# Values stationary in the attention mix of a two-layer decoder trunk, with the probabilities scaled on GpSimd first

## The reference

```
proj = h @ w_in + b_in            # 16 query heads, 2 key/value heads, head size 64
s = q k^T / 8 over the own and the previous block of 128 keys, masked to the band
mx = max(max(s), sink);  p = exp(s - mx)
p = p / (sum(p) + exp(sink - mx))
o = p v                            # per head 128 queries x 64
z = o @ w_out + b_out;  h = h + rmsnorm(z);  then rmsnorm(h) goes to the MLP
```

## Time and profile before

| | us |
|---|---|
| median of 3 runs (1154.96 to 1155.65) | 1155.17 |
| the profiled execution | 1156.1 |
| its span, first to last instruction | 1154.3 |
| attention steps: first `scores` to the first matmul of `ffn(1)` | 651.3 to 785.3 |

### The profile page before, as it was taken

How to read it: one execution, slowest core, us unless ns; L and a number is a source line. 1 busy time by engine, 2 the same in 40 slices (tenths; PEclk the granted TensorE clock), 3 DMA queues, 4 the chain that set the end, 5 groups by cost and what they waited for, 6 DMA issues and landing times.

```text
span 1154.3 us, 15362 instructions
## 1 busy us (share of the span) xinstructions
PE 1132.9 (98%) x5833; PEld 956.6 (83%) x5833; DVE 543.5 (47%) x834; ACT 431.9 (37%) x748; POOL 13.3 (1%) x22
## 2 busy tenths in 40 slices
PE   6999999999999999999999999999999999999997
PEld 6888888889888888888889988889888888888886
DVE  5434457864344344423356476646444434423344
ACT  6411225554323223323245266654332332423242
POOL 0000000000000000000000000000000000000000
PEclk9999999999999999999999999999999999999999
DMA  8232221422332333222262542002433233212241
GB/s 230 69 89 78 60 85 55 128 74 73 109 95 87 109 92 90 73 68 96 91 183 73 144 95 73 2 1 74 125 93 109 86 96 109 73 55 91 93 144 73
DMA packets 142984, 105.06 MB, mean 91 GB/s; under 512 B 22183, under 2 KB 130913, under 8 KB 142945
## 3 DMA queue, kind: packets, MB, share of 16 engines
q1 hardware_dynamic: 142944, 104.52, 30.8%
HBM read 102.41 MB, written 2.10 MB: 91 GB/s over the span
## 4 chain that ended last, share of the span: by engine, by line
PE 92%; DVE 4%; ACT 3%; DMA 1%; issue 1%; SPq 0%; DVEq 0%; ACTq 0%
PE ps L1312 18%; PE ps L1313 18%; PE ps L1314 18%; PE ps L1548 6%; PE ps L1549 6%; PE ps L1547 6%; PE ps L1651 2%; PE ps L1492 2%; PE ps L1494 2%; PE ps L1493 2%; PE ps L1377 1%; PE ps L1379 1%; PE ps L1378 1%; PE ps L1624 1%; PE ps L1635 1%; PE ps L1448 1%
## 5 line engine op out<-in xcount | busy, mean ns | idle before, releaser
L1312 PE MATMUL ps<-act_hi,w_hi 128*128 128x512 f32 (+1 forms) x1072 | 388.0, 362 | 1.4 <-DVE act_lo L848 1.4
L1313 PE MATMUL ps<-act_lo,w_hi 128*128 128x512 f32 (+1 forms) x1072 | 385.8, 360 | 0.0
L1314 PE MATMUL ps<-act_hi,w_lo 128*128 128x512 f32 (+1 forms) x1072 | 385.6, 360 | 0.0
L1312 PEld LDWEIGHTS ps<-act_hi,w_hi 128*128 128x128 f32 x1072 | 203.3, 190 | 33.4 <-DVE act_lo L848 2.2
L1314 PEld LDWEIGHTS ps<-act_hi,w_lo 128*128 128x128 f32 x1072 | 203.3, 190 | 30.1
L1313 PEld LDWEIGHTS ps<-act_lo,w_hi 128*128 128x128 f32 x1072 | 203.4, 190 | 29.7
L1547 PE MATMUL ps<-w_hi 128*128 128x512 f32 x288 | 112.0, 389 | 0.0
L1548 PE MATMUL ps<-w_lo,w_hi 128*128 128x512 f32 x288 | 112.0, 389 | 0.0
L1549 PE MATMUL ps<-w_hi,w_lo 128*128 128x512 f32 x288 | 112.0, 389 | 0.0
L671 ACT ACTIVATE arena<-ps,vecs 128x512 f32<-128x512 f32 x44 | 34.3, 780 | 188.9 <-PE ps L1314 188.9
L496 ACT CAST w_hi<-raw 128x1024 fp32r<-128x1024 f32 x71 | 73.4, 1047 | 84.3 <-PE ps L1314 45.0
(11 more groups left out here) (167 smaller groups left out, 1205.5 us busy)
## 6 DMA issues: line engine op xcount, KB each, us to landing
raw<-in_f_w_up SPq DMA_DIRECT2D x88, 512.0 KB, 4.5
raw<-in_f_w_down SPq DMA_DIRECT2D x44, 512.0 KB, 3.3
raw<-in_m_w_in SPq DMA_DIRECT2D x24, 512.0 KB, 3.8
raw<-in_m_w_out SPq DMA_DIRECT2D x8, 512.0 KB, 3.3
raw<-in_a_w_in SPq DMA_DIRECT2D x16, 256.0 KB, 4.4
raw<-in_a_w_out SPq DMA_DIRECT2D x16, 256.0 KB, 4.7
h<-in_x SPq DMA_DIRECT2D x4, 512.0 KB, 5.1
out<-h SPq DMA_DIRECT2D x3, 512.0 KB, 2.6
```

Source lines behind the costliest of these rows:

```text
L1312: nc.tensor.matmul(dst, lh, rh, start=(i == 0), stop=False)
L1313: nc.tensor.matmul(dst, lh, rl, start=False, stop=False)
L1314: last = nc.tensor.matmul(dst, ll, rh, start=False, stop=(i == n - 1))
```

## The change

`mix` is turned round: the values (128 keys x 64, a weight load with 64 columns) are stationary, and the transposed probabilities of two heads that share a key group move, 256 columns. The output of key group g goes to partitions 64g to 64g+63 of bank 4, which is the layout of `act_hi`; per step and key block there are two matmuls, g = 0 and g = 1. Queries are now along the row, so the inverse can't be applied behind the mix; POOL multiplies the probabilities by it before they are transposed, and `turn_probs` waits for POOL (`pn_done`) where it waited for ACT (`p_done`). `mixed_hi` (ACT) and `mixed_lo` (DVE) write bank 4 straight to the pair; `o_tok`, `normalised` and the 8 "out" turns are gone. `out` waits for `o_lo` of its own step, so it is listed one step earlier, `y`, `post` and `pre` keep their steps, and the norm turns lie in other steps than before. On DVE `y` now stands ahead of `masked_max`. At the end one list is left (s = 16), in which `mix(15)` stands behind `out(3, 0)`.

```diff
             if c < NB:
-                return {0: [("out", c - 2, 3), ("y", c - 2), ("turn", "out", c - 1, 0)],
-                        1: [("out", c - 1, 0), ("post", c - 2), ("turn", "out", c - 1, 1)],
-                        2: [("out", c - 1, 1), ("pre", c - 2), ("turn", "norm", c - 2, 0)],
-                        3: [("out", c - 1, 2), ("turn", "norm", c - 2, 1)]}[i]
-            if i == 0:
-                return [("out", NB - 2, 3), ("y", NB - 2), ("turn", "out", NB - 1, 0),
-                        ("turn", "out", NB - 1, 1)]
-            return [("out", NB - 1, 0), ("out", NB - 1, 1), ("post", NB - 2), ("out", NB - 1, 2),
-                    ("pre", NB - 2), ("turn", "norm", NB - 2, 0), ("turn", "norm", NB - 2, 1),
-                    ("out", NB - 1, 3), ("y", NB - 1), ("post", NB - 1), ("pre", NB - 1),
-                    ("turn", "norm", NB - 1, 0), ("turn", "norm", NB - 1, 1)]
+                return {0: [("y", c - 2), ("out", c - 1, 0), ("turn", c - 3, 1)],
+                        1: [("out", c - 1, 1), ("post", c - 2)],
+                        2: [("out", c - 1, 2), ("pre", c - 2)],
+                        3: [("out", c - 1, 3), ("turn", c - 2, 0)]}[i]
+            return [("y", NB - 2), ("out", NB - 1, 0), ("mix", AT_STEPS - 1), ("turn", NB - 3, 1),
+                    ("post", NB - 2), ("out", NB - 1, 1), ("pre", NB - 2), ("out", NB - 1, 2),
+                    ("turn", NB - 2, 0), ("turn", NB - 2, 1), ("out", NB - 1, 3), ("y", NB - 1),
+                    ("post", NB - 1), ("pre", NB - 1), ("turn", NB - 1, 0), ("turn", NB - 1, 1)]
...
+            for s in range(AT_STEPS):
+
+                b, lo = s % 2, P if s < ASTEPS else 0
+                pool.wait_ge(inv_done, s + 1)
+                nc.gpsimd.tensor_tensor(sc[:, b, :, lo:], sc[:, b, :, lo:],
+                                        asm[:, b, 5].unsqueeze(2).to_broadcast([P, AG, 2 * P - lo]),
+                                        ALU.mult).then_inc(pn_done, 1)
...
                                [:, :, lo:]).then_inc(pt_done, 1)
 
+            def mixed_hi(s):
+
+                blk, n = s // ASTEPS, s % ASTEPS
+                act.wait_ge(pv_mm, s + 1)
+                nc.scalar.copy(act_hi[:, 2 * n:2 * n + 2, blk * P:(blk + 1) * P],
...
+                elif w[0] == "mix":
+                    mixed_hi(w[1])
 
             probs(0)
-            for s in range(AT_STEPS + 2):
-                if 1 <= s <= AT_STEPS and s != ASTEPS + 1:
+            for s in range(AT_STEPS):
+                if s >= 1:
                     turned(s - 1)
-                if s >= AT_STEPS:
-
-                    for w in sorted(WORK[s], key=lambda w: s == AT_STEPS and w[0] == "y"):
-                        work(w)
-                        if w == ("post", NB - 2):
-                            split_hi(G_UP[1])
-                            split_hi(G_UP[1] + 1)
-                        if w == ("turn", "norm", NB - 2, 1):
-                            split_hi(G_UP[1] + 2)
-                        if w == ("post", NB - 1):
-                            split_hi(G_UP[1] + 3)
-                    continue
-                if s >= 1:
                     for w in WORK[s - 1]:
                         if w[0] in ("y", "post"):
                             work(w)
                 for k in OUT_SPLITS.get(s, []):
                     split_hi(G_AOUT + k)
-                if s == ASTEPS:
-                    turned(s)
+                if s >= 1:
+                    mixed_hi(s - 1)
                 if s + 1 < AT_STEPS:
                     probs(s + 1)
                 for w in WORK[s]:
                     if w[0] == "turn":
                         work(w)
+            turned(AT_STEPS - 1)
+            for w in WORK[AT_STEPS]:
+                work(w)
+                if w == ("post", NB - 2):
+                    split_hi(G_UP[1])
+                    split_hi(G_UP[1] + 1)
+                if w == ("turn", NB - 2, 1):
+                    split_hi(G_UP[1] + 2)
+                if w == ("post", NB - 1):
+                    split_hi(G_UP[1] + 3)
 
             ffn(1)
...
-            def normalised(s):
-
-                b, blk, n = s % 2, s // ASTEPS, s % ASTEPS
-                dve.wait_ge(pv_mm, s + 1)
-                dve.wait_ge(inv_done, s + 1)
-                if n == 0 and blk >= 2:
-                    dve.wait_ge(t_mm, turn_of("out", blk - 2, 1) + 1)
-                o = o_tok[:, blk % 2].rearrange("p (h d) -> p h d", d=DH)[:, n * AG:(n + 1) * AG]
-                nc.vector.tensor_tensor(
-                    o, ps[:, 4, 0:AG * DH].rearrange("p (j d) -> p j d", j=AG),
-                    asm[:, b, 5].unsqueeze(2).to_broadcast([P, AG, DH]), ALU.mult).then_inc(o_tok_done, 1)
+            def mixed_lo(s):
+
+                blk, n = s // ASTEPS, s % ASTEPS
+                dve.wait_ge(o_hi, s + 1)
+                at = (slice(None), slice(2 * n, 2 * n + 2), slice(blk * P, (blk + 1) * P))
+                nc.vector.tensor_tensor(act_lo[at], ps[:, 4, 0:2 * P].rearrange("p (t q) -> p t q", t=2),
+                                        act_hi[at].bitcast(F32), ALU.subtract).then_inc(o_lo, 1)
 
             def turn_lo(b, half):
...
+                elif w[0] == "pre":
+                    norm_pre(3 * NB + w[1], w[1])
+
+            for s in range(AT_STEPS):
+                inverse(s)
+                for w in WORK[s]:
+                    if w[0] == "y":
+                        work(w)
                 if s + 1 < AT_STEPS:
                     masked_max(s + 1)
-                if 1 <= s <= AT_STEPS:
-                    normalised(s - 1)
+                if s >= 1:
+                    mixed_lo(s - 1)
                 for k in OUT_SPLITS.get(s, []):
                     split_lo(G_AOUT + k)
...
                 if s == 1:
                     gains(2)
                 for w in WORK[s]:
-                    if w == ("pre", NB - 2):
-                        split_lo(G_UP[1])
-                    if w == ("turn", "norm", NB - 2, 0):
-                        split_lo(G_UP[1] + 1)
-                    if w == ("post", NB - 1):
-                        split_lo(G_UP[1] + 2)
...
+                    if w[0] != "y":
+                        work(w)
+            for w in WORK[AT_STEPS]:
+                if w == ("pre", NB - 2):
+                    split_lo(G_UP[1])
+                if w == ("turn", NB - 2, 0):
+                    split_lo(G_UP[1] + 1)
+                if w == ("post", NB - 1):
+                    split_lo(G_UP[1] + 2)
+                work(w)
+                if w == ("pre", NB - 1):
+                    split_lo(G_UP[1] + 3)
 
             ffn(1)
...
             def turn_probs(s):
                 b, blk = s % 2, s // ASTEPS
...
                 if s >= 1:
-                    pe.wait_ge(o_tok_done, s)
+                    pe.wait_ge(o_lo, s)
                 else:
                     pe.wait_ge(va_done, 1)
-                for j in range(AG):
-                    g = pair(s, j)[2]
-                    for kb in range(1 if blk == 0 else 0, 2):
-                        ins = nc.tensor.matmul(ps[:, 4, j * DH:(j + 1) * DH],
-                                               p_t[:, b, j, kb * P:(kb + 1) * P],
-                                               va[:, blk - 1 + kb, g * DH:(g + 1) * DH],
+                probs_of = p_t[:, b].rearrange("p (t g) k -> p g t k", g=KVH)
+                for kb in range(1 if blk == 0 else 0, 2):
+                    for g in range(KVH):
+                        gs = slice(g * DH, (g + 1) * DH)
+                        ins = nc.tensor.matmul(ps[gs, 4, 0:2 * P], va[:, blk - 1 + kb, gs],
+                                               probs_of[:, g, :, kb * P:(kb + 1) * P],
...
                 free = [q for q in range(n) if turn_bank(q) == turn_bank(n)]
                 if free:
                     pe.wait_ge(t_lo, free[-1] + 1)
-                src = o_tok[:, b % 2] if what == "out" else zn[:, b % 2]
+                if turn_bank(n) == 4:
+                    pe.wait_ge(o_lo, AT_STEPS)
                 for k in range(4):
                     ins = nc.tensor.transpose(ps[:, turn_bank(n), k * P:(k + 1) * P],
-                                              src[:, (4 * half + k) * P:(4 * half + k + 1) * P], ident[:])
+                                              zn[:, b % 2, (4 * half + k) * P:(4 * half + k + 1) * P],
+                                              ident[:])
                 ins.then_inc(t_mm, 1)
+
+            def out(b, q):
+
+                pe.wait_ge(o_lo, b * ASTEPS + q + 1)
+                if b == 0:
+                    pe.wait_ge(w_lo_done, counted(G_AOUT + 2 * q + 1))
+                if q == 0:
+                    if b == 0:
+                        pe.wait_ge(pj_used, QK_UNITS + A_UNITS + 4)
+                    else:
+                        pe.wait_ge(yb_done, b)
+                out_part(b, 6, G_AOUT, range(2 * q, 2 * q + 2), b == NB - 1)
...
```

(92 more changed lines are left out.)

26 lines of the change are left out of this document (10 added, 16 removed).

## The result

| | before | after |
|---|---|---|
| median, us | 1155.41 (4 runs, 1154.96 to 1155.95) | 1147.65 (4 runs, 1145.14 to 1148.89) |
| profiled execution | 1156.1 | 1148.89 |
| first `scores` to the first matmul of `ffn(1)` | 651.3 to 785.3 | 651.0 to 778.0 |

The ratio is 0.993, with a 95% interval of 0.9911 to 0.9948: 0.7% faster, 7.8 us in medians, 7.2 between the profiled executions. Nearly the whole gain lies in the attention, which is 7.0 us shorter.

What follows compares the result with a forecast made beforehand. PE was taken as the bound, busy 98% of the span and 92% of the chain. The terms -3.5 - 2.7 - 10.1 + 5.6 = -10.7 us took the median from 1155.17 to 1144.5 us, range 1141.5 to 1157.5.

Steps and rivals of the forecast that it cites:

- The mix: PE's mix matmuls in the attention, fewer records, running in pairs on two column halves: -10.1 us.
- lower bound: Mix records run two at a time, priced like scores at 1.06 us per long step: -10.1 us together.
- upper bound of 1.9: Mix records run one after another, 1.9 us per long step, 1.0 in the first block: loss of 1.5 us.
- rival A: In the mix, column halves run one after another: 1156.1 us, no change that can be told; chance 0.19 with rival E.
- rival E: Compiler keeps more records per matmul than counted, so PE isn't shortened: near rival A; chance 0.19 with it.
- The "out" turns: Eight groups of 4 transposes on PE go, at 0.43 us each: -3.5 us.
- The old waits: PE's five idle places in the attention go: -2.7 us.
- The end: New PE waits of 2.1 us ahead of out(3,0) and 3.5 ahead of turn(2,0), behind DVE's list: +5.6 us.
- rival C: The end costs less, y and post finding gaps, new waits under 1 us: 1139.5 us; chance 0.10.
- POOL at no cost: POOL's scaling ahead of turn_probs, 1.5 to 3.1 us, hidden by some 3.6 us left in the worst steps.
- Rival B: POOL's scaling is late, over 3.6 us, so PE waits; at 6.2 us each, 1165.5 us; chance 0.08.
- Rival D: In the mix, weight loads of the column form are not hidden, about 0.05 us each: 1162 us; chance 0.03.

Runs made afterwards that it cites:

- e2: Changed kernel with useless matmuls on PE where it waits at the end, 9 ahead of out(3,0) and 15 ahead of turn(2,0): 1144.86 us.
- e7: Changed kernel with the mix's two loops exchanged and both head groups put to the same column half: 1158.06 us.
- e10: Kernel of e3 with 4 more transposes, their result overwritten, ahead of turn_probs in every second step: 1142.37 us.
- e3: Changed kernel with DVE's list altered: block 2's bias addition ahead of mixed_lo(14), its post ahead of mixed_lo(15), the MLP split behind its pre: 1138.44 us.
- e9: Kernel of e3 without POOL's scaling, turn_probs waiting for ACT's exponentials: 1137.90 us.
- e4: Changed kernel with two more operations of the same size on POOL ahead of each scaling, their result unused: 1165.45 us.
- e8: Kernel of e3 with two more POOL operations of the scaling's size, on unused data, behind each scaling but the last: 1148.32 us.
- e11: Kernel of e3 with ACT's copy of the transposed probabilities in two halves, the first released when two heads are transposed: 1136.60 us.

## Why the prediction was right, and where it wasn't

I forecast 1144.5 us, from 1141.5 to 1157.5, and 1147.65 was measured: inside the range and on the side that was called likely, 3.15 us above the forecast. With the clock held up by useless matmuls (e2) the same kernel takes 1144.86 us, 0.4 from the forecast. By the steps of its sum, on the profiled executions:

- *The mix*, forecast -10.1 by the lower bound. Measured 12 x (1.81 - 1.02) + 4 x (0.92 - 0.58) = -10.8. The mechanism is shown by e7: with one column half the mix costs 1.87 to the next group, the upper bound of 1.9, and the gain is gone (rival A is refuted; rival E too, since a long step has 8 records of the mix, 112 in all). I took the pairing from row halves; that step, the least certain, held.
- *The "out" turns*, -3.5: e10 puts the same number back and pays 3.7 to 3.9.
- *The old waits*, -2.7: none of the five is left; PE's only waits over 0.1 us in the attention are the two new ones.
- *The end*, +5.6, as 2.1 and 3.5: measured 1.89 and 3.50, for the two operations that were named. The wait of 3.50 us begins and ends about 1.5 us later than forecast, since the slow `out(3,0)` moved PE's work and DVE's alike, so the length stayed. e3 shows that they were DVE's order and nothing else: with three edits of its list they are gone (rival C, that DVE finds gaps by itself, is refuted).
- *POOL at no cost*: e9 shows it, to within 1 us. One scaling took 1.9 us, between the bounds of 1.54 and 3.1, and the slack to `turn_probs` was 1.9 to 3.7 us in the long steps on top of it. "Some 3.6 us are left in the worst steps" came out as 3.8 in step 4 and 4.0 in step 13, but that is in part luck: in steps 10 and 14, behind `post`, which it was worked out for, 4.8 were left. Rival B was right in its mechanism, a late POOL stops PE, and with three operations (5.7 us) its rule gives some 14 us of waits, where e4 had 14.8. For its reason, that DVE works on the same memory, it had POOL four times slower; the runs show that each holds the other for whole operations, POOL in two scalings of e4, DVE in nearly every step, and that neither does so in the changed kernel (e4, e8).
- *A term that is missing: the clock.* The step that failed is the one on the end, where I counted the waits and priced what stands behind them at the full clock. `out(3,0)` took 4.50 us for 2.86, the two turns 1.62 for 0.85, `out(3,3)` 4.81 for 2.83: +4.4 us. With it the sum is -10.8 - 3.5 - 2.7 + 5.4 + 4.4 = -7.2, the difference between the profiled executions. That execution was the slowest of the four; the fastest, at a mean clock of 0.997, lies 0.6 us above the forecast, so how much of this term a run pays is chance. The trace of before gave no sign of it: its longest wait in the attention, 1.04 us, was not followed by a fall.
- *Rival D* (loads of the column form in the open) is refuted by e7: there the records start 0.216 us apart with 256 columns, twice the 0.11 of 129 columns, so no fixed time for a load is left between them. The page "TensorE: Matmul & The Clock Gate" of the Trainium skill, Part 3, The mechanism, ties the overlap of a weight load to another row group in one of its points, and in a sentence ahead of it also allows a load to the background weight buffer. The loads of one row group and one column half in e7 left no gap, so the measurement decides against the point alone; it fits the sentence, though no run here shows which buffer a load went to.

The same page, Part 1, treats an idle TensorE as what brings the lower clock. The trace agrees in kind: 3.5 us of idle was followed by a fall in four of five profiled executions, 1.9 us in one of five, and with PE kept at work (e2) there was none.

## What to carry to other kernels

A float32 matmul record with only 64 columns moving took 0.11 us here, as long as one with 129; that the weight load sets this pace is likely, but no run shows it. Make the 64-wide operand stationary, give the two halves of the output partitions to two heads, and the array runs both at once, with the output already in the layout of the next product. When a transpose or a copy is taken out of a hand-written order, walk through each engine's list again: here DVE's order of three operations was worth more (9.2 us) than the change itself (7.8 us). Count a wait of TensorE like those of 1.9 and 3.5 us here not at its own length alone but with the work behind it, which may run at half the clock; where it can't be removed, useless matmuls in it won 2.8 us.

## What the runs showed that I had not expected

- The clock: in the profiled execution it went to the lower level twice, behind waits of 1.89 and 3.50 us, and cost 4.4 us, nearly as much as the waits themselves (5.4). Equal waits were followed by a fall in some runs and not in others, which goes with a spread of 3.75 us between runs of one kernel. e2 and e3, without such waits, stay within 0.4 us. Not all of a spread is the clock, though: e9, e10 and e11, which have no such waits either, spread over 1.8, 1.5 and 1.2 us at mean clocks of 0.998 or 0.999.
- The pairing of column halves is the same in both orders that were run: one group's two matmuls ahead of the other's gave 1.02 us too.
- POOL and DVE: a DVE operation with both inputs in the shared memory that starts while POOL works lasts at least until POOL's operation is over, even at 4 numbers per partition (0.16 us alone, 1.77 us beside POOL). The other way round, a POOL operation whose turn comes while such a DVE operation is at work ends about 1 us later (2.87 us for 1.89 in e4, a pair 4.73 for 3.74 in e8). DVE's operations with one input from PSUM (0.48 us for the maxima) were as long as before. The changed kernel is spared this: its split and its subtraction take 1.22 and 0.16 us throughout, since POOL's 1.9 us fall beside DVE's maxima and its idle time. "GPSIMD Engine Reference" of the Trainium skill, section 1, names such a contention for DVE instructions with two inputs in this memory; the trace agrees, with the 1.77 us above.
